# Second block, one slot of the attention pipeline: low halves of a turned weights' tile ahead of the weight conversion on VectorE

## The chip, the cores and the metric

The kernel runs on one core of one Trainium2 chip. The metric is the device time of one execution in microseconds (us).

## The reference, cut to what matters

Two blocks run one after the other on 256 tokens of width 1024, all in float32. The first block (gated linear attention, a dense feed-forward part, windowed attention, a mixture of eight experts) isn't touched. The second block puts 16 learned tokens ahead of the 256, so it has 272 rows, and has two layers of two kinds of attention side by side:

```python
dq, dk, dv, dg, fq, fk, fv, ff, fg = jnp.split(proj, split_points, axis=-1)
...
# four differential heads: two softmaxes and one difference each
p = jax.nn.softmax(s, axis=-1)
a = p[:, :, 0] - lam * p[:, :, 1]
do = einsum('bhqk,bhkd->bhqd', a, v)
do = rmsnorm(do, subln_gain[l], SUBLN_EPS) * (1.0 - lam_init)
do = do * jax.nn.silu(dg)
...
# eight forgetting heads: a decay is added to the scores
s = s + cq[..., None] - cum_logf[:, :, None, :]
p = jax.nn.softmax(s, axis=-1)
fo = einsum('bhqk,bhkd->bhqd', p, v) * jax.nn.silu(fg)
...
h = h + jnp.concatenate([do, fo], axis=-1) @ w_out[l]
```

## The kernel before, in words

**High and low halves.** Float32 products are made from three matmuls: each operand is split into a rounded high half and the remainder, its low half. ScalarE writes the high half, then VectorE the low half, which needs the high half and the source. So it goes with the weight pieces (`whi` by `hi_to`, L179; `wlo` by `lo_to`, L189; 128 x 2048 each), with the turned attention weights (`aTh`, L2427; `aTl`, L2684) and with the gated head outputs (`xh`, L2376; `xl`, L2599). Weight pieces are loaded by SyncE's queue into four raw buffers and converted into three pairs of buffers in a fixed order; SyncE issues the next load into a raw buffer once its `wlo` is done.

**Units and slots.** A layer of the second block works through *units*: one tile of query rows and one pair of heads. The first `nd` units are differential, the next `nd` are forgetting units (`nd` is 12 in layer one, 8 in layer two). `att_order` (L1861) lays them out as a software pipeline of slots `u`: in a slot TensorE makes the scores of unit `u` (L2220, L2221 end them), turns the weights of unit `u - 2` (transposes, L2239) and multiplies those of unit `u - 3` with the values. VectorE takes the scores out of PSUM and finds their maximum (L2642, L2644), ScalarE exponentiates (L2407) and, in a forgetting unit, scales (L2417). Every engine runs the same `att_order` with its own functions, so the order of calls in it is each engine's program order; where an engine has nothing to do, it passes a function that does nothing. Between these calls `take(beside, ...)` puts steps of the projections: `fv`, then the turning (L2178) and gating of the four differential heads (`gate`, `rp`, L2594; `out_low`, `xl`, L2599), then the output projection in steps `out(n)`.

**Slot `nd + 3`.** Here the last differential units are done, and `heads` (L2650) scales their outputs into `oxd`: the differential heads come through. On VectorE the slot reads: reciprocals (L2656) and scores of the new unit, `heads`, the weight conversion `low()`, the low half `aTl` of the turned weights of unit `nd + 1`, then `finish(nd)`, which writes the gated output `fw` (L2700). `N_BESIDE_F` gives this slot no step beside. The call `low()` does something on VectorE alone (`convert`, L189); the other engines pass `never` in that place.

**Who reads what.** `aTl` of a unit frees the PSUM banks that TensorE's next transposes write: in `turned(u)` on TensorE the wait is

```python
pe.wait_ge(t_lo.at(l, u - 1) if u > nd else a_cp.at(l, nd - 2 + a))
```

The first step of the output projection, `out(0)`, waits for the low halves of all four gated heads:

```python
pe.wait_ge(W.lo(i), f_xl.at(l, unit_f(t, 3)) if part else y(3),
           gated.at(l, 2 + n) if n < 2 else o_add.at(l, *OUT[n - 2]))
```

The piece that `low()` converts in slot `nd + 3` is the second half (columns 512 to 1023) of the first part of `w_out`.

Of the kernel before, what the change touches and what calls it, by code (L numbers as in the profile page):

```python
# [196 lines left out]
def run(steps):  # L197
    for _ in steps:
        pass
# [8 lines left out]
def body(nc, ctx, I, out):  # L208
# [1643 lines left out]
    def take(gen, n):  # L1852
        for _ in range(n):
            next(gen, None)
# [6 lines left out]
    def att_order(l, beside_d, beside_f, normal, scores, heads, low, turned, values, weights, powers, evict, finish, high):  # L1861

        units = units_of[l]
        nu = len(units)
        nd = nu // 2
        take(beside_d, 2)
        for u in range(nu + 3):
            if u == nd:
                run(beside_d)
            if u < nd:  # L1870
                beside, n = beside_d, (N_BESIDE_D - 2) * (u + 1) // nd - (N_BESIDE_D - 2) * u // nd
            else:
                beside, n = beside_f, N_BESIDE_F[l][u - nd]
            if 0 <= u - 1 < nu:
                normal(u - 1)
            if u < nu:
                scores(u)
            if 4 <= u < nd + 4 and units[u - 4][2] == 3:
                heads(u - 4)
            low()  # L1880
            take(beside, n // 2)
            if 0 <= u - 2 < nu:
                turned(u - 2)
            take(beside, n - n // 2)
            if 0 <= u - 3 < nu:
                values(u - 3)
            if 0 <= u - 1 < nu:
                weights(u - 1)
            if u < nu:
                powers(u)  # L1890
            evict()
            if 0 <= u - 3 < nu:
                finish(u - 3)
            high()
        low()
        run(beside_f)
# [87 lines left out]
    def make_layer(l):  # L1984
# [103 lines left out]
        def pe(pe):  # L2088
# [153 lines left out]
            def values(u):  # L2242
# [12 lines left out]
                else:  # L2255
# [4 lines left out]
                    for kt in range(NKT[nk]):  # L2260
                        ins = mm3(pe, to, fvh[:, kt, c], fvl[:, kt, c], aTh[:, u % 2, kt, :, 0:m], aTl[:, u % 2, kt, :, 0:m],
                                  kt == 0, kt == NKT[nk] - 1)
                ins.then_inc(pv2.end(l, u))

            att_order(l, beside_d(), beside_f(), nothing, scores, nothing, never, turned, values, nothing, nothing, never, nothing,
                      never)
            for n in range(len(OUT) - 2, len(OUT)):
                out(n)

        def act(act):  # L2270
# [158 lines left out]
            def finish(u):  # L2429
                (qi, qo, m, nk), kind, i = units[u]  # L2430
                if kind == "f":
# [7 lines left out]
                                 accum_out=st[0:m, 16 + qi * 4 + i:17 + qi * 4 + i]).then_inc(o_sq.end(l, qi, i))  # L2439

            att_order(l, beside_d(), beside_f(), normal, nothing, nothing, never, turned, nothing, nothing, powers,
                      lambda: evict_of(pending), finish, convert)
            act.wait_ge(hd.at(l, 2), s_table.at("swa", 1) if l == 0 else s_table.at("b0"))
# [6 lines left out]
        def dve(dve):  # L2450
# [243 lines left out]
            def finish(u):  # L2694
                (qi, qo, m, nk), kind, i = units[u]
                if kind == "f":
# [7 lines left out]
                    if u == nu - 1:  # L2704
                        f_low(u)

            att_order(l, beside_d(), beside_f(), normal, scores, heads, convert, turned, nothing, weights, nothing,
                      lambda: evict_of(pending), finish, due)
            for n in range(len(OUT) - 3, len(OUT)):
# [165 lines left out]
```

## Time and profile before

| | |
|---|---|
| median of 3 runs | 1737.73 us (1737.05 to 1737.78) |
| the profiled execution, its own time | 1740.94 us |
| its span | 1739.1 us |
| TensorE matmul (PE) busy | 1622.5 us, 93% |
| VectorE (DVE) busy | 1228.3 us, 71% |
| ScalarE (ACT) busy | 1036.3 us, 60% |
| GpSimd (POOL) busy | 59.9 us, 3% |
| slot `nd + 3`, layer one / layer two | about 1467 / 1679 us from the span's start |

The span is one execution as the profiler took it; all starts below are counted from its beginning. Busy shares are means over the whole span and say little of a single slot. An instruction's record can begin a few hundredths of a microsecond before that of the one ahead of it on its engine ends, since neighbours overlap, so what an instruction takes of its engine's queue is read from start to start. In a timeline the square brackets at a row's end give the idle time of the engine just before it and the operation that ended it. The chain of waits lists what ended last, followed back from the last instruction: a row in it had nothing to spare.

### The profile page before, as it was taken

How to read it: one execution, taken by the hardware profiler on the slowest of the kernel's cores; microseconds unless marked ns; L12 is line 12 of the kernel's file. 1: busy time of each engine (PE TensorE's matmuls, PEld its weight loads, DVE VectorE, ACT ScalarE, POOL GpSimd, SP SyncE). 2: the span in 40 equal slices, each digit the busy share in tenths (PEclk: the TensorE clock that was granted, in tenths of full speed). 3: DMA queues.
4: the chain of work that ended last, by engine and by line, in shares of the span. 5: the costliest groups of instructions: out<-in, count | busy, mean ns of one | idle time of the engine just before them, and what ended most of it. 6: DMA issues, size and time to landing. Idle time of an engine off the chain costs nothing.

```text
span 1739.1 us, 21544 instructions
## 1 busy us (share of the span) xinstructions
PE 1622.5 (93%) x8649; PEld 1360.0 (78%) x8649; DVE 1228.3 (71%) x1298; ACT 1036.3 (60%) x1244; POOL 59.9 (3%) x62
## 2 busy tenths in 40 slices
PE   5999999997889999999999999999987989889987
PEld 5877888787768888888888888888867877688866
DVE  3655555368558888888888888888884566555665
ACT  4644544355547767776776777677774456454463
POOL 0000000022000000000000000000000200003000
PEclk9999999998969999999999999999998999999999
DMA  7422555551339999999999999999994543236410
GB/s 248 146 97 97 194 178 185 190 200 61 103 119 336 390 320 352 331 357 368 336 331 314 400 322 357 334 335 381 322 307 120 126 121 97 49 82 137 123 48 37
DMA packets 133081, 389.31 MB, mean 224 GB/s; under 512 B 8695, under 2 KB 14267, under 8 KB 132845
## 3 DMA queue, kind: packets, MB, share of 16 engines
q1 hardware_dynamic: 132692, 387.15, 65.2%
q8 instruction: 70, 1.15, 0.3%
q10 hardware_dynamic: 280, 0.69, 0.1%
q14 instruction: 39, 0.31, 0.1%
HBM read 386.77 MB, written 1.05 MB: 223 GB/s over the span
## 4 chain that ended last, share of the span: by engine, by line
PE 79%; DVE 9%; ACT 7%; issue 3%; DMA 1%; ACTq 0%; SPq 0%; DVEq 0%; POOL 0%
PE psum L356 25%; PE psum L358 24%; PE psum L357 24%; DVE wlo L189 4%; ACT whi L179 3%; PE psum L1533 1%; PE psum L1585 1%; DMA c<-in_c_dram 1%; DVE Ss L1229 1%; PE psum L2253 1%; DVE mx L1234 0%; ACT hh L1645 0%; PE psum L415 0%; PE psum L2098 0%; PE psum L2239 0%
## 5 line engine op out<-in xcount | busy, mean ns | idle before, releaser
L189 DVE TENSOR_TENSOR wlo<-raw,whi 128x2048 fp32r<-128x2048 f32 (+1 forms) x286 | 629.6, 2213 | 224.2 <-ACT whi L179 223.5
L179 ACT ACTIVATE whi<-raw 128x2048 fp32r<-128x2048 f32 (+1 forms) x286 | 525.8, 1847 | 236.7 <-PE psum L358 236.7
L356 PE MATMUL psum<-whi,xh 128*128 128x512 f32 (+1 forms) x1280 | 498.4, 389 | 18.2 <-DVE xl L2599 9.9
L358 PE MATMUL psum<-whi,xl 128*128 128x512 f32 (+1 forms) x1280 | 486.4, 380 | 0.0
L357 PE MATMUL psum<-wlo,xh 128*128 128x512 f32 (+1 forms) x1280 | 485.5, 379 | 0.0
L356 PEld LDWEIGHTS psum<-whi,xh 128*128 128x128 f32 x1280 | 242.6, 190 | 75.2 <-issue 13.3
L358 PEld LDWEIGHTS psum<-whi,xl 128*128 128x128 f32 x1280 | 242.3, 189 | 49.7
L357 PEld LDWEIGHTS psum<-wlo,xh 128*128 128x128 f32 x1280 | 243.1, 190 | 45.9 <-issue 0.2
L189 DVE TENSOR_TENSOR wlo<-raw_more,whi 128x2048 fp32r<-128x2048 f32 (+1 forms) x94 | 204.0, 2177 | 39.7 <-ACT whi L179 38.4
L179 ACT ACTIVATE whi<-raw_more 128x2048 fp32r<-128x2048 f32 (+1 forms) x94 | 171.4, 1827 | 53.8 <-PE psum L358 53.8
L356 PE MATMUL psum<-xh,whi 128*128 128x256 f32 (+2 forms) x552 | 165.5, 300 | 24.4 <-DVE wlo L189 22.8
L356 PE MATMUL psum<-whi,hh 128*128 128x512 f32 x440 | 176.8, 402 | 1.1 <-DVE hl L974 1.1
L357 PE MATMUL psum<-wlo,hh 128*128 128x512 f32 x440 | 173.8, 395 | 0.0
L358 PE MATMUL psum<-whi,hl 128*128 128x512 f32 x440 | 173.8, 395 | 0.0
L358 PE MATMUL psum<-xh,wlo 128*128 128x256 f32 (+2 forms) x552 | 159.9, 290 | 0.0
L357 PE MATMUL psum<-xl,whi 128*128 128x256 f32 (+2 forms) x552 | 159.9, 290 | 0.0
L356 PEld LDWEIGHTS psum<-xh,whi 128*128 128x128 f32 (+1 forms) x552 | 105.4, 191 | 30.1 <-DVE wlo L189 23.5
L357 PEld LDWEIGHTS psum<-xl,whi 128*128 128x128 f32 (+1 forms) x552 | 105.4, 191 | 0.8
L358 PEld LDWEIGHTS psum<-xh,wlo 128*128 128x128 f32 (+1 forms) x552 | 105.1, 190 | 0.6
L356 PEld LDWEIGHTS psum<-whi,hh 128*128 128x128 f32 x440 | 82.7, 188 | 20.1 <-issue 1.3
L358 PEld LDWEIGHTS psum<-whi,hl 128*128 128x128 f32 x440 | 82.7, 188 | 19.8
L357 PEld LDWEIGHTS psum<-wlo,hh 128*128 128x128 f32 x440 | 82.8, 188 | 17.5
(363 smaller groups left out, 1513.8 us busy)
## 6 DMA issues: line engine op xcount, KB each, us to landing
raw<-in_moe_w_down_dram SPq DMA_DIRECT2D x58, 1024.0 KB, 7.6
raw<-in_moe_w_gate_dram SPq DMA_DIRECT2D x43, 1024.0 KB, 6.3
raw<-in_moe_w_up_dram SPq DMA_DIRECT2D x41, 1024.0 KB, 6.0
raw_more<-in_moe_w_down_dram SPq DMA_DIRECT2D x30, 1024.0 KB, 7.3
raw<-in_w_in_dram SPq DMA_DIRECT2D x28, 1024.0 KB, 8.0
raw_more<-in_moe_w_up_dram SPq DMA_DIRECT2D x23, 1024.0 KB, 6.2
raw_more<-in_moe_w_gate_dram SPq DMA_DIRECT2D x21, 1024.0 KB, 6.9
raw<-in_moe_w_up_dram SPq DMA_DIRECT2D x23, 768.0 KB, 4.9
```

The costliest lines, as they stand in the source:

```text
L179: act.e.activation(self.whi[:, i % self.ns, 0:kt * n], self.place[self.slots[i]][:, 0:kt * n], ACT.Copy, scale=1.0).then_inc(self.s_hi)
L189: dve.e.tensor_tensor(self.wlo[:, i % self.ns, 0:kt * n], self.place[self.slots[i]][:, 0:kt * n], self.whi[:, i % self.ns, 0:kt * n].bitca ...
L356: pe.e.matmul(o, lh, rh, start=start, stop=False)
L357: pe.e.matmul(o, lh, rl, start=False, stop=False)
L358: return pe.e.matmul(o, ll, rh, start=False, stop=stop)
L1229: ins = dve.e.scalar_tensor_tensor(Ss[:, u % 4, i, :], dst, -float(np.float32(slope[head(n, i)])), psum[:, bk[i // 2], (i % 2) * T:(i % 2) ...
L1533: ins = pe.e.matmul(psum[:, b, 0:N], half[:, j, k * 128:(k + 1) * 128], Pm[:, j, :], start=j == 0 and half is xnh, stop=j == 1 and half is ...
L1585: ins = pe.e.transpose(psum[:, b, j * 128:(j + 1) * 128], hid[:, c:c + 128], ident)
L2253: ins = pe.e.matmul(psum[0:m, 4, c], aT[:, u % 2, kt, 0:m], vvd[:, kt, c], start=kt == 0, stop=kt == NKT[nk] - 1)
```

## The change

In slot `nd + 3` the call `low()` is made behind `turned(u - 2)` and not ahead of it; in all other slots it stays. The first `take` of the slot has no step to take, so nothing else lies between the two.

```diff
                 scores(u)
             if 4 <= u < nd + 4 and units[u - 4][2] == 3:
                 heads(u - 4)
-            low()
+            if u != nd + 3:
+                low()
             take(beside, n // 2)
             if 0 <= u - 2 < nu:
                 turned(u - 2)
+            if u == nd + 3:
+                low()
             take(beside, n - n // 2)
             if 0 <= u - 3 < nu:
                 values(u - 3)
```

VectorE's program in slot `nd + 3` of layer one, before (`Sx` are the scores and weights, `s` their maxima and reciprocals; the brackets name the semaphores waited for, and `swa_top` there counts ScalarE's writing of `aTh`):

```order
L2642 TENSOR_TENSOR Sx<-psum,c_95 128x544 [waits swa_pv,att_turned,att_scores]
L2644 TENSOR_REDUCE s_107<-Sx 128x2 [waits att_top]
L2650 TENSOR_TENSOR oxd<-psum,st 128x512 [waits att_pv,heads_rstd]
L189 TENSOR_TENSOR wlo<-raw,whi 128x2048 [waits w_hi,w_passed,w_landed3]
L2684 TENSOR_TENSOR aTl<-psum,aTh 128x768 [waits swa_top]
L2700 TENSOR_TENSOR fw<-psum,sg 64x128 [waits gates,att_pv]
```

The same place in the changed program, whose lines below L1880 have numbers higher by 3:

```order
L2645 TENSOR_TENSOR Sx<-psum,c_95 128x544 [waits swa_pv,att_turned,att_scores]
L2647 TENSOR_REDUCE s_107<-Sx 128x2 [waits att_top]
L2653 TENSOR_TENSOR oxd<-psum,st 128x512 [waits att_pv,heads_rstd]
L2687 TENSOR_TENSOR aTl<-psum,aTh 128x768 [waits swa_top]
L189 TENSOR_TENSOR wlo<-raw,whi 128x2048 [waits w_hi,w_passed,w_landed3]
L2703 TENSOR_TENSOR fw<-psum,sg 64x128 [waits gates,att_pv]
```

`aTl` and `wlo` have changed places, with the waits that each had. The same happens once in layer two, and the programs of the other four engines are the same as before.

## Rows read from the trace of the kernel before

**Rows 1.** Page, chain that ended last, share of the span by engine.

```profile
PE 79%; DVE 9%; ACT 7%; issue 3%; DMA 1%; ACTq 0%; SPq 0%; DVEq 0%; POOL 0%
```

**Rows 2.** Waits of PE, 1465 to 1500 us: total us, times, longest.

```profile
PE psum L356 <- DVE xl L2599: 4.7, 1, 4.7
PE psum L2239 <- DVE aTl L2684: 2.3, 1, 2.3
```

**Rows 3.** Chain of waits, 1467 to 1485 us: start, us, what.

```profile
1470.06 0.85 DVE wlo L189
...
1472.17 0.95 DVE aTl L2684
...
1480.97 0.80 ACT aTh L2427
...
1483.66 0.45 DVE xl L2599
...
1484.20 0.76 PE psum L356
```

**Rows 4.** Timeline of DVE, 1455 to 1482 us: start, us, engine, line, operation.

```profile
1464.57 0.96 DVE L2684 TENSOR_TENSOR aTl<-psum,aTh 128x768 fp32r<-128x768 f32 x1 [2.99 <-ACT aTh L2427]
...
1469.38 0.68 DVE L2650 TENSOR_TENSOR oxd<-psum,st 128x512 f32<-128x512 f32 x1
1469.97 2.28 DVE L189 TENSOR_TENSOR wlo<-raw,whi 128x2048 fp32r<-128x2048 f32 x1
1472.17 0.95 DVE L2684 TENSOR_TENSOR aTl<-psum,aTh 128x768 fp32r<-128x768 f32 x1
1473.04 0.58 DVE L2700 TENSOR_TENSOR fw<-psum,sg 64x128 f32<-64x128 f32 x2
...
1476.39 0.96 DVE L2684 TENSOR_TENSOR aTl<-psum,aTh 128x768 fp32r<-128x768 f32 x1 [1.19 <-ACT aTh L2427]
```

**Rows 5.** Timeline of ACT, the same stretch.

```profile
1463.72 0.81 ACT L2427 ACTIVATE aTh<-psum 128x768 fp32r<-128x768 f32 x1 [2.76 <-PE psum L2239]
...
1470.05 0.79 ACT L2427 ACTIVATE aTh<-psum 128x768 fp32r<-128x768 f32 x1
```

**Rows 6.** Timeline of PE, 1467 to 1501 us.

```profile
1473.27 0.96 PE L2239 MATMUL psum<-cst,Sx 128*16 128x128 f32 x6 [2.26 <-DVE aTl L2684]
...
1478.19 0.82 PE L2239 MATMUL psum<-cst,Sx 128*16 128x128 f32 x6
...
1484.20 0.76 PE L356 MATMUL psum<-whi,xh 128*128 128x512 f32 x1 [4.67 <-DVE xl L2599]
...
1500.51 0.48 PE L356 MATMUL psum<-whi,xh 128*128 128x512 f32 x1
```

**Rows 7.** Timeline of SyncE's queue, 1466 to 1486 us.

```profile
1472.28 0.37 SPq L155 DMA_DIRECT2D raw<-in_w_in_dram  x1
```

**Rows 8.** Timelines of layer two: DVE, then ACT, then PE.

```profile
1680.71 0.68 DVE L2650 TENSOR_TENSOR oxd<-psum,st 128x512 f32<-128x512 f32 x1
1681.31 2.28 DVE L189 TENSOR_TENSOR wlo<-raw,whi 128x2048 fp32r<-128x2048 f32 x1
1683.50 0.95 DVE L2684 TENSOR_TENSOR aTl<-psum,aTh 128x768 fp32r<-128x768 f32 x1
1684.37 0.58 DVE L2700 TENSOR_TENSOR fw<-psum,sg 64x128 f32<-64x128 f32 x2
...
1681.38 0.79 ACT L2427 ACTIVATE aTh<-psum 128x768 fp32r<-128x768 f32 x1
...
1695.39 0.77 PE L356 MATMUL psum<-whi,xh 128*128 128x512 f32 x1 [5.24 <-DVE xl L2599]
```

**Rows 9.** Busy time by stretch: PE, PEld, DVE, ACT, POOL, granted clock, DMA.

```profile
1473.30:1477.20 3.90, 3.90 (x21) 3.31 (x22) 2.60 (x7) 2.27 (x5) 0.00 (x0) 0.56 0.89 268
...
1484.20:1487.50 3.30, 3.30 (x8) 2.62 (x9) 0.00 (x0) 0.22 (x2) 0.00 (x0) 0.51 0.02 5
...
1695.40:1699.30 3.90, 3.90 (x10) 3.08 (x11) 0.00 (x0) 0.23 (x2) 0.00 (x0) 0.53 0.02 4
```

## The prediction

> **What bounds the kernel now.** I read the chain of waits over the whole span first. TensorE carries 79% of it, VectorE 9% and ScalarE 7% [rows 1]. So a microsecond of VectorE counts only in the few places where the chain runs over it, and the question is whether the edited slot is one of them.
>
> Then I read who waited for whom on TensorE around that slot in the first layer. Two waits stand there: 2.3 us for a turned weights' low half (`aTl`), and 4.7 us for `xl`, the low half of the last gated differential head, which the first output projection reads [rows 2]. The reader is to see that the second is the larger, and comes later.
>
> The third view, the chain of waits in that stretch alone, settles which engine matters. From 1470.06 it goes from `wlo` to `aTl`, and through VectorE and ScalarE alone to `xl` at 1483.66 and TensorE's first output-projection matmul at 1484.20 [rows 3], so in this stretch TensorE only waits. Its own work between 1470 and 1484 isn't on the chain: the engine stands still for 4.67 us before that matmul [rows 6]. What TensorE gets earlier in this stretch is only more waiting later; what VectorE gets later is paid in full.
>
> **The change, layer one.** Nothing is added or removed. In slot `nd + 3`, VectorE now runs `aTl` (L2684) before `wlo` (L189), once per layer. The DMA queue and the other three engines keep their orders.
>
> Before: the scaling of the heads (`oxd`) runs 1469.38 to 1470.06. `wlo` starts at 1469.97, the starts overlapping the end of the one ahead by some 0.08, and `aTl` follows at 1472.17, `fw` at 1473.04 [rows 4]. So `wlo` takes 1472.17 − 1469.97 = 2.20 us of the queue and `aTl` takes 1473.04 − 1472.17 = 0.87. VectorE has no gap here.
>
> After: `aTl` needs the high half `aTh`, which ScalarE makes from 1470.05 to 1470.84 [rows 5]. ScalarE's order is untouched, and so is what it waits for there. VectorE is free at 1470.06 and has to wait. On an earlier unit `aTh` ended at 1463.72 + 0.81 = 1464.53 [rows 5] and `aTl` started at 1464.57 [rows 4], 0.04 later. So `aTl` starts at 1470.84 + 0.04 = 1470.88, `wlo` at 1470.88 + 0.87 = 1471.75, `fw` at 1471.75 + 2.20 = 1473.95. It was 1473.04: **0.91 us later**. Bounds: counted by ends the new hole is 1470.84 − 1470.06 = 0.78; if the new order of the pair costs another 0.1 of start-up (the overlap of 0.08 lost once), it is 1.0.
>
> This is a hole that `wlo` used to fill. The Trainium skill, page "PSUM — Partial Sum Buffer", section on engine and sequencer instructions, says that the queues of ScalarE and VectorE are strict FIFO; by that rule `wlo`, whose inputs are there, may not pass the waiting `aTl`. An engine that let it pass would make the sum zero, and the rule speaks against the change. In the rows an `aTl` that waited 2.99 us had nothing run ahead of it [rows 4].
>
> What follows `fw` on VectorE is moved by the 0.91: the normalising sums, the scores of the next unit, the first gated head. ScalarE's `xh` waits for that head, the next `aTh` stands behind `xh` in ScalarE's queue, and the next `aTl` waits for it (1476.39, after 1.19 us of waiting [rows 4]). No step of the chain up to `xl` at 1483.66 is TensorE's; that `aTh` at 1480.97 is again its link [rows 3]. So no slack of TensorE takes any of it up.
>
> What gets earlier: `aTl` ends at 1471.83 instead of 1473.12. TensorE's next transposes start some 0.15 after that, at 1471.98 instead of 1473.27 [rows 6], 1.29 us earlier. But the transposes after those (1478.19 before [rows 6]) need the next `aTl`, which now ends at 1476.39 + 0.96 + 0.91 = 1478.26, so they start at about 1478.4, and the 1.29 us are gone before the output projection, which starts at 1484.20 + 0.91 = 1485.11.
>
> By the Trainium skill, page "Perfetto Trace Analysis", section "Optimization Strategies", one speeds up what blocks the critical path whenever the matmul engine idles. Read with the wait of 2.26 us alone, that would give −1.29 us in this layer. The chain [rows 3] disagrees.
>
> Costed at nothing: `wlo`'s own lateness. It ends 1.78 us later (1474.03, not 1472.25). Its piece is the second half of the first output part, and TensorE's first matmul on it is the fourth output step at 1500.51 [rows 6]: 26 us of cover, less 0.9. SyncE's load into the freed buffer was issued at 1472.28, right when `wlo` ended [rows 7], and goes at some 1474.1; it fills a piece read only by the next layer. Without that cover each would cost at most its 1.8 us.
>
> After 1484.20 VectorE and ScalarE wait for TensorE, so all later steps move with it.
>
> **Layer two.** The same rows repeat: `oxd` from 1680.71 to 1681.39, `wlo` at 1681.31, `aTl` 1683.50, `fw` 1684.37, and `aTh` from 1681.38 to 1682.17 [rows 8]. The new start of `fw` is 1682.17 + 0.04 + 0.87 + 2.19 = 1685.27 against 1684.37: **0.90 us later**, bounds 0.78 and 1.0. TensorE waited 5.24 us before its output projection here [rows 8], so the earlier transposes buy nothing in this layer either. No load hangs on this `wlo`, since there is no piece left to load.
>
> **Sum.** 0.91 + 0.90 = 1.81 us. The profiled execution had a span of 1739.10 and a time of 1740.94; it becomes 1740.9 and 1742.8. The runs shown are lower, median 1737.73, so the time forecast is 1737.73 + 1.81 = **1739.5 us**, 0.10% more. A measurement of this kernel tells about 0.2%, 3.5 us, from no change, so the forecast is "the same".
>
> **Rivals.**
> A, *TensorE's wait for `aTl` is the bound* (5%). Then both layers gain what `aTl` gains: 1.29 and, in layer two, 1683.50 − 1682.21 = 1.29, together 2.6 us, so 1735.1. If the shorter pause also kept the clock up, the stretch 1473.3 to 1477.2, granted 0.56 [rows 9], would give back 3.9 × 0.44 = 1.7 us, taken for layer two as well, and the time is 1731.7. For it: the waits named in the trace are exactly on this operation. Against it: the 4.67 and 5.24 us of idleness that follow.
>
> B, *slower by more than 0.2%: the clock* (6%). After the pause of 4.67 us TensorE runs 3.3 us at a mean grant of 0.51, and after that of 5.24 us it runs 3.9 us at 0.53 [rows 9], which is the 1.2 GHz level for nearly all of it. These stretches are on the chain, at a cost of 3.3 × 0.49 = 1.6 and 3.9 × 0.47 = 1.8 us. My pauses grow by about 0.7. If each low stretch grew to twice its length, it would add 3.4: 1737.73 + 1.81 + 3.4 = 1742.9. It decides from 1.7 us of added loss on. Against it: the pause in layer two is 0.57 longer than in layer one, and the stretch cost only 0.2 more. The Trainium skill, page "TensorE: Matmul & The Clock Gate", section "Why this matters for your kernels", warns of idle gaps between bursts for this reason.
>
> C, *no cost* (7%): the hole is not there or is swallowed, because one of the later waits on VectorE (1.19 us at 1476.39 [rows 4]) is in truth for something that doesn't move with `fw`: 1737.7. For it: that wait alone is longer than 0.91. Against it: the `aTh` it waits for is on the chain in the same form a unit later (1480.97 [rows 3]), behind ScalarE's work on what VectorE made just before.
>
> **How the numbers follow.** The forecast takes 82%. Its own range is +1.6 to +2.0 by the bounds, with up to half of B's added loss on top (+3.6 in all) and the runs' scatter of 0.7. The range for 8 in 10 reaches down to C, 1737.4, and up to 1741.3; A, B and the tails lie outside. Faster by over 0.2% needs A with its clock, 3%. Slower by over 0.2% is B, 6%. Within: 91%.
>
> **What would show it.** In the timeline of VectorE after: `oxd`, a wait of about 0.8 us for `aTh`, `aTl`, `wlo`, with `fw` starting 3.89 us behind the end of `oxd`, against 2.98 before. TensorE's wait for the first `aTl` falls from 2.3 to about 1.0, and its pause before the output projection grows to 5 us and more. The distance from `oxd`'s start to the output projection's first matmul was 14.82 us in layer one and 14.68 in layer two; it should be 15.7 and 15.6. I am wrong if that distance stays or shrinks, or if the matmuls behind it stay at the lower level for much over 4 us.

## The result, and the profile after

The changed kernel takes **1743.54 us** (median of 10 runs, 1739.83 to 1747.86), the kernel before 1737.65 in the same comparison (10 runs, 1736.20 to 1744.19). The ratio is 1.0026, with a 95% interval of 1.0017 to 1.0035: slower by 4.5 us, between 3.0 and 6.1. The two medians lie 5.9 us apart, inside that interval too; the text goes by the ratio, here and below. The forecast was 1739.5 us, 1.8 us slower, in a range up to 1741.3. The time lies above the range, and the loss is some two and a half times the forecast. A second timing of the same kernel (`after_a`, below) gave 1.0034, 1.0021 to 1.0048.

The profiled execution took 1742.32 us, its span is 1740.5 us; the page's chain by engine is as before but for "issue", 4% for 3% [rows 1]:

```profile
span 1740.5 us, 21544 instructions
...
PE 79%; DVE 9%; ACT 7%; issue 4%; DMA 1%; ACTq 0%; SPq 0%; DVEq 0%; POOL 0%
```

**The hole is there, in the place and at the size forecast.** Timeline of VectorE in slot `nd + 3` of layer one, which answers to [rows 4] (start, us, engine, line, operation, and in brackets the idle time ahead):

```profile
1468.44 0.68 DVE L2653 TENSOR_TENSOR oxd<-psum,st 128x512 f32<-128x512 f32 x1
1469.93 0.96 DVE L2687 TENSOR_TENSOR aTl<-psum,aTh 128x768 fp32r<-128x768 f32 x1 [0.81 <-ACT aTh L2430]
1470.81 2.28 DVE L189 TENSOR_TENSOR wlo<-raw,whi 128x2048 fp32r<-128x2048 f32 x1
1473.01 0.58 DVE L2703 TENSOR_TENSOR fw<-psum,sg 64x128 f32<-64x128 f32 x2
...
1476.37 0.96 DVE L2687 TENSOR_TENSOR aTl<-psum,aTh 128x768 fp32r<-128x768 f32 x1 [1.19 <-ACT aTh L2430]
```

From the end of `oxd` (1469.12) to `fw` it is 3.89 us, as forecast, for 2.98 before. The wait of 1.19 us further down is unchanged, so nothing swallowed the delay. In layer two the same, with [rows 8] as its counterpart; the last row is TensorE's:

```profile
1680.28 0.68 DVE L2653 TENSOR_TENSOR oxd<-psum,st 128x512 f32<-128x512 f32 x1
1681.78 0.96 DVE L2687 TENSOR_TENSOR aTl<-psum,aTh 128x768 fp32r<-128x768 f32 x1 [0.82 <-ACT aTh L2430]
1682.65 2.28 DVE L189 TENSOR_TENSOR wlo<-raw,whi 128x2048 fp32r<-128x2048 f32 x1
1684.85 0.58 DVE L2703 TENSOR_TENSOR fw<-psum,sg 64x128 f32<-64x128 f32 x2
...
1695.89 0.77 PE L356 MATMUL psum<-whi,xh 128*128 128x512 f32 x1 [4.74 <-DVE xl L2602]
```

Two distances serve as measures from here on. **The way in** goes from the start of `oxd` to the first matmul of the output projection. **The way out** goes from that matmul to the next `fw` on VectorE, which waits for TensorE's 12 projection matmuls and the value product behind them. The way in was forecast at 15.7 and 15.6 us and is 1484.17 − 1468.44 = 15.73 and 1695.89 − 1680.28 = 15.61.

**TensorE's pauses**, which answer to [rows 6]: the wait for the first `aTl` is gone, three shorter ones stand in its place, and the pause before the projection is there still. It is 0.24 us shorter and not 0.7 longer: the last transposes ahead of it, at half clock now, take 1.44 us, where they took 0.82 [rows 6].

```profile
1471.04 0.81 PE L2242 MATMUL psum<-cst,Sx 128*16 128x128 f32 x6 [0.97 <-ACT Sx L2410]
...
1474.33 0.34 PE L356 MATMUL psum<-fkh,fqh 64*128 64x144 f32 x2 [0.88 <-DVE Sx L2645]
...
1477.47 1.44 PE L2242 MATMUL psum<-cst,Sx 128*16 128x128 f32 x6 [1.65 <-DVE aTl L2687]
...
1484.17 0.77 PE L356 MATMUL psum<-whi,xh 128*128 128x512 f32 x1 [4.43 <-DVE xl L2602]
```

**What the forecast lacks stands behind the projection's first matmul.** Before, the way out was 1489.82 − 1484.20 = 5.62 us in layer one and 5.82 in layer two. Now `fw` starts at 1490.93 and the way out is 6.76 us, and 6.71 in layer two. Busy time by stretch (columns as in [rows 9]; the last number but two is the granted clock) shows why: TensorE works there at half clock for 5.7 us, where it was about 3.2 us before [rows 9]. In layer two it is 5.6 us, for 3.7 before.

```profile
1476.20:1484.17 7.97, 2.27 (x9) 1.48 (x10) 6.49 (x15) 4.41 (x15) 0.00 (x0) 0.50 0.21 79
1484.17:1489.90 5.73, 5.72 (x15) 4.57 (x16) 0.00 (x0) 0.22 (x2) 0.00 (x0) 0.50 0.01 3
1489.90:1500.00 10.10, 9.98 (x69) 8.33 (x69) 7.65 (x16) 6.09 (x16) 0.00 (x0) 1.00 0.29 44
```

So there are two terms in this profile: the way in, 0.91 + 0.93 = 1.84 us, and the way out, 1.14 + 0.89 = 2.03 us. The experiments ask what each really costs, and where the second comes from.

### The profile page after: what moved, and what is told of

It reads as the page before. It is cut to its first block, busy times and chain, and to the rows that moved or that the text cites. A ratio compares the mean times of both kernels' runs of the same rounds, so it can differ in the third digit from the quotient of the medians.

```text
span 1740.5 us, 21544 instructions
## 1 busy us (share of the span) xinstructions
PE 1622.1 (93%) x8649; PEld 1359.7 (78%) x8649; DVE 1228.0 (71%) x1298; ACT 1035.9 (60%) x1244; POOL 59.9 (3%) x62
## 3 DMA queue, kind: packets, MB, share of 16 engines
HBM read 386.77 MB, written 1.05 MB: 223 GB/s over the span
## 4 chain that ended last, share of the span: by engine, by line
PE 79%; DVE 9%; ACT 7%; issue 4%; DMA 1%; ACTq 0%; SPq 0%; DVEq 0%; POOL 0%
PE psum L356 25%; PE psum L358 24%; PE psum L357 24%; DVE wlo L189 4%; ACT whi L179 3%; PE psum L1533 1%; PE psum L1585 1%; DMA c<-in_c_dram 1%; DVE Ss L1229 1%; DVE mx L1234 1%; PE psum L2256 1%; ACT hh L1645 0%; PE psum L2101 0%; PE psum L2242 0%; PE psum L2147 0%
```

## The experiments

All times are against the kernel before, run on the same chip in the same comparison; ratios are turned into microseconds with 1737.7. Each kernel was timed 5 to 12 times. The two distances are from one profiled execution of each kernel.

| kernel | way in, layers one and two | way out | time against before, 95% interval (us) |
|---|---|---|---|
| before | 14.82, 14.68 | 5.62, 5.82 | |
| the change | 15.73, 15.61 | 6.76, 6.71 | +4.5 (+3.0 to +6.1) |
| `hole` | 15.74, 15.60 | 6.92, 6.87 | +3.8 (+1.9 to +5.7) |
| `hold` | 15.70, 15.55 | 5.60, 6.95 | +3.5 (+0.9 to +6.1) |
| `one_layer` | 15.73, 14.69 | 6.91, 5.85 | +1.2 (−0.7 to +3.1) |
| `split` | 15.00, 14.87 | 5.79, 5.80 | +0.2 (−1.6 to +1.9) |
| `hole2` | 16.81, 16.66 | 6.29, 6.18 | +2.6 (+0.9 to +4.3) |
| `warm_before` | 14.78, 14.65 | 5.71, 5.71 | −0.2 (−1.9 to +1.6) |
| `warm_after` | 15.69, 15.56 | 4.16, 4.16 | −4.7 (−6.4 to −3.0) |
| `fill_before` | 14.79, 14.65 | 4.15, 4.15 | −3.1 (−4.7 to −1.6) |
| `fill_after` | 15.70, 15.56 | 4.16, 4.14 | −1.4 (−3.0 to +0.2) |
| `late_low` | 13.54, 13.41 | 6.30, 6.68 | −4.0 (−6.1 to −1.9) |
| `late_both` | 12.64, 12.50 | 6.64, 6.55 | −4.5 (−6.2 to −3.0) |
| `fill_late` | 13.06, 12.46 | 4.04, 4.14 | −6.6 (−8.7 to −4.3) |

### `hole`: the hole without the new order

```diff
+            if u == nd + 3:
+                dve.wait_ge(t_hi.at(l, u - 2))   # on VectorE only
             low()
```

> The order of before, but VectorE waits for aTh ahead of wlo in slot nd + 3, so the hole of 0.8 us is there and TensorE's transposes come 0.9 us later than before, not 1.3 us earlier. Theory (two terms: the hole, 0.9 us a layer, and a longer stretch at the lower clock, 1.1 us a layer, which comes from TensorE's earlier work): from oxd's start to the output projection's first matmul 15.7 and 15.6 us in the two layers, from that matmul to the next fw 5.6 and 5.8 us as before, time 1.8 us over before. Rival 1 (the low stretch's length is chance, or grows with the pause): 6.8 us to the next fw, time 4 us over before. Rival 2 (a late wlo or a late load costs): wlo is 0.9 us late here, so half of the excess over 1.8 us stays, some 3 us over before.

```profile
1466.67 0.68 DVE L2653 TENSOR_TENSOR oxd<-psum,st 128x512 f32<-128x512 f32 x1
1468.17 2.29 DVE L189 TENSOR_TENSOR wlo<-raw,whi 128x2048 fp32r<-128x2048 f32 x1 [0.82 <-ACT aTh L2430]
```

In this timeline of VectorE the same hole stands ahead of `wlo` instead of `aTl`, and TensorE waits 3.17 us for `aTl` where the change took that wait away. The way in is that of the change, and so is the way out. My theory, that the clock's term came from TensorE's *earlier* work, falls here: this kernel has its work later and pays as much.

### `hold`: the new order, TensorE kept at its old rhythm

```diff
                 pe.wait_ge(a_at(u), s_exp2.at(l, u))
+                if u == nd + 2:
+                    pe.wait_ge(W.lo(P[("fv", l)] + NS))
```

> The order of the change, and TensorE's transposes of unit nd + 2 are held back until the moved wlo is done, so that TensorE rests and works about as before (start some 4.6 us behind oxd's start, 3.9 before). Theory (two terms): the hole stays, 15.7 and 15.6 us to the output projection; the clock's term goes, 5.6 to 5.8 us from its first matmul to the next fw, time 1.8 us over before, which is less than the change although a wait was added. Rival 1 (chance): as the change, 6.8 us and 4 to 6 us over before. Rival 2 (late wlo or late load): as the change too, since both are as late here.

The way in is that of the change. The way out is 5.60 in one layer and 6.95 in the other, in a single execution. So one execution can have both lengths; TensorE's work of the ten microseconds before doesn't settle which, since it is nearly the same in both layers. The time, +3.5 us, does not tell the theories apart.

### `one_layer` and `split`: half the change, and the hole filled

`one_layer` makes the change with `l == 0` only. `split` converts 704 columns of `wlo` ahead of `aTl`, the other 1344 behind:

```diff
-            if u != nd + 3:
-                low()
+            if u != nd + 3:
+                low()
+            else:
+                part(0, 704)
...
             if u == nd + 3:
-                low()
+                part(704, 2048)
```

> The change in the first layer alone. Theory (two terms, the same in each layer): layer one as in the change (15.7 and 6.8 us), layer two as before (14.7 and 5.8 us), time 2.0 to 2.9 us over before. Rival 2 (the late load of the next layer's piece, which only layer one has): nearly the whole excess of the change, 4 us or more. Rival 3 (only layer two costs more than the hole): 0.9 us over before.

> In slot nd + 3 the first 704 of wlo's 2048 columns are converted ahead of aTl, the rest behind it: the hole is filled, and aTl is as early as in the change. Theory (two terms): from oxd's start to the output projection 14.9 and 14.8 us (0.1 for one more instruction), but the clock's term stays with TensorE's early work, 6.8 us from its first matmul to the next fw, time 2.2 us over before. Rival 1 (the low stretch grows with the pause on VectorE's side, or is chance): no change from before, within 0.5 us. Rival 2 (late wlo): as before plus next to nothing, since wlo ends 0.9 us late.

`one_layer` pays in layer one alone, in the way in and in the way out. Its time is within scatter of none, and below the 2.0 expected at least; its interval rules out that the late load of layer one carries the whole. `split` has `aTl` exactly as early as the change (1.49 us behind `oxd`), no hole, and no cost:

```profile
1466.00 0.68 DVE L2666 TENSOR_TENSOR oxd<-psum,st 128x512 f32<-128x512 f32 x1
1466.60 0.88 DVE L187 TENSOR_TENSOR wlo<-raw,whi 128x704 fp32r<-128x704 f32 x1
1467.49 0.96 DVE L2700 TENSOR_TENSOR aTl<-psum,aTh 128x768 fp32r<-128x768 f32 x1
1468.37 1.55 DVE L187 TENSOR_TENSOR wlo<-raw,whi 128x1344 fp32r<-128x1344 f32 x1
1469.84 0.58 DVE L2716 TENSOR_TENSOR fw<-psum,sg 64x128 f32<-64x128 f32 x2
```

The rows, VectorE's timeline, have no bracket: no idle time. This run settles two things. The early `aTl` buys nothing (rival A), and it does no harm either: both terms hang on the hole.

### `warm_before` and `warm_after`: TensorE with work to do in its pauses

```diff
+            def busy(bank, n):
+                wh, _ = W.views(P[("out", l, 0, 0)])
+                pe.wait_ge(W.lo(P[("out", l, 0, 0)]))
+                for _ in range(n):
+                    pe.e.matmul(psum[:, bank, :], wh[:, 0, 0:128], wh[:, 1, :], start=True, stop=True)
...
+                if u == nd + 2:
+                    busy(4, 6)
                 pe.wait_ge(a_at(u), s_exp2.at(l, u))
...
+                pe.wait_ge(f_w.at(l, nd))
+                busy(5, 10)
                 for n in range(len(OUT) - 2):
                     out(n)
```

> The kernel before, and TensorE runs matmuls whose results nobody reads where it would stand still: 6 ahead of the transposes of unit nd + 2 and 10 ahead of the output projection's first matmul, on banks that are free there. Theory (the level of the clock behind the pause is part of this stretch's price): the distance from oxd's start to the output projection stays 14.8 and 14.7 us, the first matmuls behind it run at the full level, 4.0 to 4.4 us to the next fw instead of 5.6 to 5.8, time 2 to 3.5 us under before. Rival (the level doesn't matter, or falls in spite of the added work): 5.6 us or more to the next fw, time as before or longer.

> The change, with the same added matmuls. If the change costs the hole and some clock, and the added work takes the clock's part away, this lies the hole's 1.8 us over warm_before, with 15.7 and 15.6 us to the output projection and 4.0 to 4.4 us from there to the next fw. If the excess over the hole (4.5 - 1.8 = 2.7 us) has nothing to do with the clock in this stretch, it lies 4 us or more over warm_before.

TensorE's timeline in `warm_before` shows why the same 16 matmuls did nothing there. The 10 ahead of the projection ran at full clock, were done in 2.52 us, and left a pause of 3.03 us. The projection began at full clock, and 0.4 us later (0.55 in layer two) the clock fell. The timeline, then busy time by stretch:

```profile
1475.89 2.52 PE L2198 MATMUL psum<-whi 128*128 128x512 f32 x10
1481.45 0.50 PE L356 MATMUL psum<-whi,xh 128*128 128x512 f32 x1 [3.03 <-DVE xl L2609]
```

```profile
1481.45:1481.87 0.42, 0.42 (x2) 0.38 (x3) 0.00 (x0) 0.27 (x2) 0.00 (x0) 0.94 0.00 0
1481.87:1485.27 3.40, 3.40 (x10) 2.62 (x9) 0.00 (x0) 0.00 (x0) 0.00 (x0) 0.51 0.02 5
```

In `warm_after` they ran at half clock nearly to their end, took 4.34 us and left 0.40 us; the clock came up while they ran:

```profile
1476.67 4.34 PE L2201 MATMUL psum<-whi 128*128 128x512 f32 x10
1481.41 0.51 PE L356 MATMUL psum<-whi,xh 128*128 128x512 f32 x1 [0.40 <-DVE xl L2612]
```

The price of the clock on the way out is the difference: 5.71 us against 4.16, or 1.55 us a layer. As a pair the two don't measure the hole, since one was filled and the other wasn't. Nor do the distances explain `warm_after`'s time: by them it should gain 1.4 us on the kernel before, and it gains 4.7 (3.0 to 6.4). Where the other 3.3 us come from stays open.

### `fill_before` and `fill_after`: the pauses filled in both

As above, with 16 matmuls ahead of the projection, 3 ahead of the scores of unit `nd + 5` and 5 ahead of the transposes of unit `nd + 3`.

> The kernel before with unread matmuls in all of TensorE's pauses of this stretch: 6 ahead of the transposes of unit nd + 2, 3 ahead of the scores of unit nd + 5, 5 ahead of the transposes of unit nd + 3, 16 ahead of the output projection. In warm_before a pause of 3.0 us was left and the level fell all the same; here about 0.7 to 1.5 us is left. Theory (the level behind the pause is part of the stretch's price, and follows from the last pause's length): 14.8 and 14.7 us to the output projection, 4.0 to 4.3 us from there to the next fw, time 3 us under before. Rival (the level doesn't matter for the time): as before.

> The change with the same filling: 15.7 and 15.6 us, 4.0 to 4.3 us. With the clock's part gone from both, this lies over fill_before by what the hole costs alone. Theory: 1.8 us. Rival (the change costs 2 to 3 us beyond the hole in a way that has nothing to do with this stretch's clock): 4 us or more. Rival (the earlier aTl is worth something once TensorE is warm, as warm_after, 4 us under before, might suggest): 0 or less.

Busy time by stretch, `fill_before` and then `fill_after`, from the projection's first matmul on; the granted clock is 1.00 in both:

```profile
1482.67:1486.80 4.13, 4.13 (x23) 3.47 (x23) 0.00 (x0) 0.27 (x2) 0.00 (x0) 1.00 0.00 0
```

```profile
1479.91:1484.00 4.09, 4.09 (x23) 3.42 (x23) 0.00 (x0) 0.26 (x2) 0.00 (x0) 1.00 0.00 0
```

The ways out are equal to 0.02 us, the ways in differ by the 0.91 of the hole. By the distances `fill_before` should gain 3.2 us (1.47 + 1.67, and 0.06 on the way in), and it gains 3.1. `fill_after` should gain 1.4, and gains 1.4. So with the way out at full clock in both, the change costs 1.7 us over `fill_before`, near the forecast's 1.8, with an uncertainty of about 2. That leaves some 2.7 of its 4.5 us for the clock, as an estimate uncertain by nearly 3. The distances are firmer than the times here: `warm_after` has those of `fill_after` to 0.02 us and is 3.3 us faster against the kernel before.

### `hole2`: twice the hole

VectorE waits for `s_exp2.at(l, nd + 3)` too, ahead of `wlo`.

> The order of before, and VectorE waits ahead of wlo until ScalarE's exponentials of the slot are done, which makes the hole twice as long: 1.8 us a layer. Both theories: 16.6 and 16.5 us from oxd's start to the output projection. Theory 1 (the hole costs itself and nothing more, the excess in the change's and hole's times is scatter of the clock): 3.6 us over before. Theory 2 (every microsecond of hole costs some two, since it lengthens TensorE's pause): 7 us or more over before.

The way in grows by 1.99 and 1.98 us, but the way out is 0.6 us shorter than in `hole`, and the time is no more than `hole`'s. The loss doesn't grow with the hole; the 7 us of theory 2 are ruled out. The rise of the clock stayed about where it is in `hole` (21.5 and 21.1 us behind `oxd`, for 21.9 and 21.6), so the later projection ran a shorter part at half clock. That is 0.6 us a layer; by the distances the kernel should still be 5.0 us slower than before, and it is 2.6 (0.9 to 4.3). The rest was not found.

### Four more executions: is the longer way out the change's or the execution's?

The two kernels unchanged, in fresh executions: `after_a`, `after_b`, `before_a`, `before_b`.

> The change once more, for a second execution of it in the profile and a second timing beside before. If the longer way from the output projection's first matmul to the next fw belongs to the change, it is 6.7 us and more in both layers again, and the time 4 to 5 us over before. If it belongs to the execution (where the low stretch lies against the program), it lies anywhere from 5.6 to 6.9 us, and the time is the hole's 1.8 us over before plus scatter.

> A third execution of the change: 6.7 us and more in both layers if it belongs to the change; anywhere from 5.6 to 6.9 us if to the execution. The distances from oxd to the output projection 15.7 and 15.6 us by both.

> A second execution of the kernel before: 5.6 to 5.9 us from the output projection's first matmul to the next fw in both layers, if the short way belongs to this kernel; anywhere from 5.6 to 6.9 us if to the execution. 14.8 and 14.7 us from oxd to the output projection by both.

> A third execution of the kernel before: 5.6 to 5.9 us again if the short way belongs to this kernel, anywhere up to 6.9 us if to the execution.

| | way in | way out |
|---|---|---|
| `before_a` | 14.83, 14.69 | 5.80, 5.91 |
| `before_b` | 14.83, 14.69 | 5.67, 5.80 |
| `after_a` | 15.73, 15.59 | 5.50, 6.89 |
| `after_b` | 15.74, 15.60 | 6.94, 6.87 |

With the first profiles, the kernel before went out in 5.62 to 5.91 us six times out of six; the changed one in 6.71 to 6.94 five times and in 5.50 once. Add layer two of `one_layer` and both of `split` to the former, and `hole`, `hold` and layer one of `one_layer` to the latter: nine of nine short with a way in of up to 15.0 us, nine of eleven long with 15.6 or 15.7. It belongs to the change, though not in every execution.

Finely cut stretches give the moment at which the clock rises. In the three executions of the kernel before, it lies 18.0 to 18.6 us behind the start of `oxd`, and in the short way out of `after_a` it lies 18.8 behind, although the projection began 0.9 us later there. Busy time by stretch, `before_a` and then `after_a`, from the projection's first matmul to the rise, and past it:

```profile
1479.55:1483.20 3.65, 3.65 (x9) 2.88 (x10) 0.00 (x0) 0.22 (x2) 0.00 (x0) 0.50 0.02 4
1483.20:1485.30 2.10, 2.10 (x16) 1.79 (x14) 0.00 (x0) 0.00 (x0) 0.00 (x0) 1.00 0.00 0
```

```profile
1479.95:1483.00 3.05, 3.05 (x7) 2.46 (x8) 0.00 (x0) 0.22 (x2) 0.00 (x0) 0.50 0.02 5
1483.00:1485.40 2.40, 2.40 (x17) 2.01 (x15) 0.00 (x0) 0.00 (x0) 0.00 (x0) 1.00 0.00 0
```

The rise doesn't keep its distance from the matmuls. The traces of all kernels without added matmuls hold 26 ways out, whose projections start from 12.5 to 16.8 us behind `oxd`. The rise lies 17.8 to 19.0 us behind `oxd` in 15 of them, 21.1 to 21.9 us behind in 11, and in none between. A projection that began by 15.0 us got the earlier moment 13 times out of 13. One that began at 15.55 us or later got the later moment 11 times out of 13, and then the clock stayed down until 5.6 to 6.2 us behind the first matmul (in `hole2`, whose projections are later still, 4.4 to 4.7). Twice, in `after_a` and in `hold`, it got the earlier one, and the way out was as short as 5.50 and 5.60. That is a step of 1.1 us for a delay of 0.9.

The mean ways out of the three executions each are 5.70 and 5.84 before, 6.40 and 6.82 after. That makes 1.7 us in all, and with the way in 3.5 us, inside the interval of the first timing (3.0 to 6.1) and just short of the second (3.6 to 8.3).

The two distances aren't the whole account, though, since stretches at half clock further on come and go as well. From layer one's `fw` to layer two's `oxd` the kernel before takes 190.9 us in all three executions; the changed one takes 190.9 in `after_a`, and 189.3 or 189.4 in the two others, behind the long ways out. From layer two's `fw` to the end of the span it is 37.9 to 38.0 us before, and 37.9, 39.2 and 39.2 after. Busy time by stretch, 41.5 us behind layer one's `oxd` and 38.5 us behind layer two's, `before_b` and then `after_b`:

```profile
1509.55:1513.55 4.00, 4.00 (x11) 3.16 (x12) 1.79 (x7) 1.48 (x8) 0.00 (x0) 0.57 0.96 178
1717.96:1721.96 4.00, 4.00 (x22) 3.38 (x21) 2.61 (x6) 0.35 (x2) 0.00 (x0) 1.00 0.01 4
```

```profile
1507.65:1511.65 4.00, 2.27 (x18) 1.76 (x12) 3.66 (x11) 1.43 (x8) 0.00 (x0) 1.00 0.54 83
1716.59:1720.59 4.00, 3.76 (x12) 3.09 (x13) 2.75 (x7) 0.80 (x2) 0.00 (x0) 0.57 0.00 0
```

A stretch at half clock is gone in layer one, and one is new in layer two. From `oxd` to `oxd` the change therefore costs only 0.6 us (211.8 to 212.2 against 211.3 to 211.5), less than its hole, and from there to the end 2.8 us. Together it is 3.3 us in the mean of three executions each (273.2 against 269.9): 1.8 for the ways in, 1.5 for the clock in all that follows. The first timing says 4.5, with 3.3 inside its interval. Which of the later stretches follow from the change and which from the execution was not tried. They matter for the times: within the ten timed runs of the change, the two with a mean clock of 0.975 took 1739.8 and 1740.2 us, the eight with 0.969 to 0.971 took 1741.8 to 1747.9.

### `late_low` and `late_both`: the conversion out of the slot

Both kernels skip `low()` in slots `nd + 3` to `nd + 5` and call it in slot `nd + 5` behind `take(beside, n - n // 2)`, where VectorE has waited 5.7 us for TensorE. `late_both` moves ScalarE's `whi` of that piece there as well:

```diff
-            low()
+            if not nd + 3 <= u <= nd + 5:
+                low()
             take(beside, n // 2)
             if 0 <= u - 2 < nu:
                 turned(u - 2)
             take(beside, n - n // 2)
+            if u == nd + 5:
+                late()      # ScalarE in late_both: W.hi_to(act, P[("fv", l)] + 1 + NS)
+                low()
```

> The wlo of slot nd + 3 moves out of the slot altogether, to slot nd + 5 behind the last gated head, where VectorE stands still for 5.7 us waiting for TensorE. The hole of 0.8 us ahead of aTl is there as in the change, but 2.2 us of wlo are gone from the chain. By the rows fw starts 1.29 us earlier than before: 13.5 and 13.4 us from oxd's start to the output projection, time 2.6 us under before. If the moved wlo is in the way of the next fw, or if the pause's length decides and not VectorE's chain, no gain.

> ScalarE's whi and VectorE's wlo of slot nd + 3 both move to slot nd + 5, behind the last gated head, where both engines wait for TensorE. Then aTh doesn't stand behind whi, the hole ahead of aTl is gone and so are the 2.2 us of wlo: 12.6 and 12.5 us from oxd's start to the output projection. By the rows 4.4 us under before; if the pause's clock adds to it, between 3 and 6. Against late_low it gains 1.8 us, which is the hole again, taken out on ScalarE's side. If the hole is not what the change costs, no difference from late_low.

```profile
1466.70 0.68 DVE L2662 TENSOR_TENSOR oxd<-psum,st 128x512 f32<-128x512 f32 x1
1467.30 0.95 DVE L2696 TENSOR_TENSOR aTl<-psum,aTh 128x768 fp32r<-128x768 f32 x1
1468.17 0.58 DVE L2712 TENSOR_TENSOR fw<-psum,sg 64x128 f32<-64x128 f32 x2
...
1480.70 2.29 DVE L189 TENSOR_TENSOR wlo<-raw,whi 128x2048 fp32r<-128x2048 f32 x1 [1.46 <-ACT whi L179]
1485.98 0.59 DVE L2712 TENSOR_TENSOR fw<-psum,sg 64x128 f32<-64x128 f32 x2 [3.00 <-PE psum L358]
```

In `late_both`'s timeline of VectorE, `aTl` follows `oxd` without a wait, and `wlo` lies in the pause before the next `fw` and still leaves 3.00 us of it. The ways in came out as expected to 0.1 us in both. The ways out got longer, by 0.7 to 1.0 us in both kernels, since the rise of the clock stayed where it was (17.8 to 19.0 us behind `oxd`). The distances alone would give 1.0 us for `late_low` and 2.6 for `late_both`; the times gained are 4.0 and 4.5, so here too the distances of one execution don't hold all of it. The 1.8 us between the two kernels stand in the ways in (0.90 and 0.91); the times, 0.5 us apart and each uncertain by 2, can't show them.

### `fill_late`: `late_both` with the pauses filled

> late_both with the filling of fill_before. The distances are 12.6 and 12.5 us, from there to the next fw 4.0 to 4.4 us; time 7.5 us under before if the two gains add up. If the filling comes in TensorE's way now that its pauses are shorter: later than 12.6 us and no gain over late_both.

The ratio is 0.9962 (0.9950 to 0.9975), median 1730.15 us against 1737.57: **6.6 us faster than before**, from 4.3 to 8.7, and so faster than both kernels. Only 5 runs stand behind it. In layer two the way in is 12.46 and the way out 4.14 us; both gains are there. In layer one the filling reached into the projection, which began 0.4 us late for it (13.06 where `late_both` has 12.64), so a little less of it would do there.

## Why the prediction was wrong

- **What bounds the kernel** held. The chain ran over VectorE and ScalarE in this stretch, and `split`, with the same early `aTl` and no hole, was as fast as before. TensorE's wait of 2.26 us, the largest thing the change removed, was worth nothing (rival A, 5%).
- **The hole** held in place and size: 0.91 and 0.90 forecast, 0.91 and 0.93 in the profile, 1.7 us in time (uncertain by 2) with the clock up on the way out in both kernels. The rule of the Trainium skill, page "PSUM — Partial Sum Buffer", section "Engine vs sequencer instructions", that VectorE's queue is strict FIFO, agrees with the 0.81 us for which `wlo` stood ready behind the waiting `aTl`.
- **Costed at nothing**, the late `wlo` and the late load: `split` ends `wlo` 1.05 us later behind `oxd` than before (the change 1.78), with the load behind it, and costs nothing measurable.
- **"After 1484.20 … all later steps move with it"** is the step that failed. It put the clock at nothing. The steps moved, and took 1.1 us longer on the way: TensorE's matmuls behind the pause stayed at half clock for 5.7 us where it had been 3.2 (5.6 for 3.7 in layer two). It was rival B, with 6%. I had set its price at a doubled stretch, 3.4 us in all; it was 1.7 us on the ways out of six profiles, 1.5 over all that follows in them, and some 2.7 by the times.
- **The argument against B** was at fault. Layer two's pause was 0.57 us longer and cost only 0.2 more, and I took that for the slope. The two rows were two samples from the short side of a step. A longer pause wasn't even what happened: it fell from 4.67 to 4.43 us, and from 5.24 to 4.74. What counted was how late TensorE's work resumed, by 15.0 us behind `oxd` or from 15.55 on.
- **The range** should have held this. Half of B's loss was put on top of the forecast, but only as a tail, where both layers take the same step in most executions. The chance of "slower" was far too low at 6%.

## What to carry to other kernels

Before an instruction is moved ahead of another on an in-order engine, ask whether its input will be there: an early place for an operation whose input comes 0.8 us later turns the work that used to cover this time into a delay of everything behind it. And where the delayed chain ends in TensorE's restart after a pause, the delay isn't the whole price. The level of the clock behind the pause comes on top, in steps rather than in proportion, so look at it in several executions before calling a term small.

## What the runs showed of the hardware

The moment at which TensorE's clock rose after the pause didn't follow the matmuls that restarted it. Without added matmuls it lay at one of two places behind `oxd`, 17.8 to 19.0 us or 21.1 to 21.9 us, for restarts anywhere from 12.5 to 16.8 us behind it. The Trainium skill, page "TensorE: Matmul & The Clock Gate", section "What's actually happening", warns that the number of slow matmuls differs from run to run of one kernel and needn't be modelled. The changed kernel agrees (7 to 17 matmuls between restart and rise); the kernel before does not, with 8 or 9 matmuls in all six of its ways out. What fixes the two places against the program was not tried.

Useless matmuls kept the clock up where they reached near enough to the real ones: with 3.03 us of pause left (`warm_before`) it fell 0.4 us into the projection, with 0.5 to 1.9 us left (`fill_before`, `fill_after`) it stayed up throughout. The latter two also had more such matmuls in the pauses ahead, and which of the two counts was not tried.
